# Projection stage of a one-core decoder step: value units on ScalarE, top-k rounds moved, first index scores earlier

## What is computed

```python
h = rmsnorm(x, g_mix)
proj = h @ w_in        # q_d,k_d,v_d | q_s,k_s,v_s | q_i,k_i,w_i | gates
q_d, k_d, q_s, k_s = rope(rmsnorm(per head of 64), pos)
q_i, k_i = rope(q_i, pos), rope(k_i, pos);  w_i = w_i * H_IDX ** -0.5
dots  = einsum('bqhd,bkd->bqhk', q_i, k_i) * DH_IDX ** -0.5
score = einsum('bqhk,bqh->bqk', relu(dots), w_i)    # causal
_, idx = top_k(score, 128)                          # of 512 (513) keys
```

## Time and profile before

| | us |
|---|---|
| median of 3 runs | 1186.04 (1186.01 to 1187.33) |
| the profiled execution | 1185.78 |
| its span, first to last instruction | 1184.0 |
| TensorE / VectorE / ScalarE / GpSimd busy | 1032.5 / 440.0 / 239.7 / 298.8 |
| projections, until TensorE's first instruction of the next stage | 289.28 |

### The profile page before, as it was taken

One profiled execution on the slowest core, in us unless ns is written; L12 is line 12 of the kernel. 1 busy time (PEld: TensorE's weight loads), 2 busy tenths in 40 slices (PEclk: granted clock), 3 DMA queues, 4 the chain that ended last, 5 costly groups with the idle time before them and its releaser, 6 DMA issues. The chain is left out here.

```text
span 1184.0 us, 16123 instructions
## 1 busy us (share of the span) xinstructions
PE 1032.5 (87%) x5989; PEld 576.3 (49%) x5989; DVE 440.0 (37%) x1213; ACT 239.7 (20%) x542; POOL 298.8 (25%) x262
## 2 busy tenths in 40 slices
PE   6998999988999999998999499999787777777775
PEld 3644443444777777332555355544444343444442
DVE  3635878786565574322334211111111011101220
ACT  2111212211444545301033201111100110011101
POOL 1033312441554434001000012322212221222111
PEclk9999999999999999998999789999999999999998
DMA  6232022107476444898391899999999999999991
GB/s 201 91 111 81 1 99 98 54 37 236 141 242 209 133 134 156 303 325 298 135 420 65 319 345 398 397 396 391 407 407 401 398 402 404 400 398 401 406 389 52
DMA packets 82465, 304.27 MB, mean 257 GB/s; under 512 B 23138, under 2 KB 27362, under 8 KB 70226
## 3 DMA queue, kind: packets, MB, share of 16 engines
q1 hardware_dynamic: 64658, 273.47, 60.6%
q0 software_dynamic: 9824, 16.98, 5.0%
q10 hardware_dynamic: 7904, 12.78, 3.0%
HBM read 290.09 MB, written 29.72 MB: 270 GB/s over the span
## 5 line engine op out<-in xcount | busy, mean ns | idle before, releaser
L383 PE MATMUL p_z<-k_w,k_xT 128*128 128x512 f32 (+2 forms) x528 | 212.3, 556 | 3.5 <-DVE p_t L584 3.4
L383 PEld LDWEIGHTS p_z<-k_w,k_xT 128*128 128x128 f32 (+1 forms) x528 | 93.1, 191 | 107.4 <-issue 106.7
L842 PE MATMUL a_G<-k_xT,k_w 128*128 128x260 f32 x512 | 127.3, 393 | 0.0
L2007 DVE TENSOR_TENSOR e_hid<-e_hid,e_G 128x256 f32<-128x256 f32 x32 | 13.5, 421 | 270.4 <-ACT e_hid L1920 263.2
L1925 ACT ACTIVATE e_y<-e_Y,x_share 64x512 f32<-64x512 f32 x64 | 43.7, 684 | 313.3 <-PE e_Y L1810 304.4
L842 PEld LDWEIGHTS a_G<-k_xT,k_w 128*128 128x128 f32 x512 | 93.2, 192 | 26.7 <-issue 13.8
L937 POOL TENSOR_TENSOR k_x<-k_x 128x512 f32<-128x512 f32 x64 | 80.5, 1272 | 89.6 <-DVE k_side L1003 66.0
L2048 POOL DMA_INDIRECT out_y_p<-e_y,x_table x32 | 45.1, 1408 | 202.8 <-ACT e_y L1925 144.1
L152 POOL DMA_INDIRECT k_rows<-token_rows,x_table x32 | 31.4, 981 | 179.1 <-PE e_TX L1790 169.6
L2012 DVE TENSOR_TENSOR e_hid<-e_hid,e_U 128x256 f32<-128x256 f32 x32 | 13.5, 421 | 126.1 <-PE e_U L1796 126.1
L1213 PE MATMUL g_ring<-k_oT,k_w 128*128 128x512 f32 x128 | 59.9, 614 | 0.0
(11 more groups left out here) (354 smaller groups left out, 1492.1 us busy)
## 6 DMA issues: line engine op xcount, KB each, us to landing
k_w<-in_w_in SPq DMA_DIRECT2D x11, 2048.0 KB, 8.5
k_xT<-in_w_down SPq DMA_DIRECT2D x11, 2048.0 KB
x_page<-in_w_down SPq DMA_DIRECT2D x10, 2048.0 KB
x_w_out<-in_w_down SPq DMA_DIRECT2D x10, 2048.0 KB
k_w<-in_w_gate SPq DMA_DIRECT2D x8, 2048.0 KB
k_w<-in_w_up SPq DMA_DIRECT2D x8, 2048.0 KB
k_oT<-in_w_gate SPq DMA_DIRECT2D x8, 2048.0 KB
k_side<-in_w_up SPq DMA_DIRECT2D x8, 2048.0 KB, 44.7
```

What stands on the lines that cost most here:

```text
L383: last = nc.tensor.matmul(z[u % 3][0:p, 0:WIDTH[k]], s.xT[:, j, 128 * i:128 * i + p], s.w[:, c % 2, j, 0:WIDTH[k]], start=j == 0, stop=j = ...
L842: last = nc.tensor.matmul(G[u % 2][:, 0:HT], s.w[:, q % 2, j, 128 * c:128 * c + 128], s.xT[:, j, HT * h:HT * h + HT], start=j == 0, stop=j ...
```

## The change

1. A value unit is copied out of its bank by ScalarE instead of VectorE (the sample unit straight into its row by four copies), and counted by a new semaphore `v_copied`. TensorE and SyncE wait for it where a value unit is meant; `z_free` now counts the other units only (`worked_before`).
2. A normalised prompt unit runs two rounds between its sums and its scaling, one behind the cosine product, none behind the unit.
3. A value prompt unit runs `2600 // (width + 128)` rounds (6, 5 or 4 at 256, 384, 512 columns), one less in a unit of `extras`.
4. The eight scores of t = 1 are made in units 10 and 11, four in each; those of t = 2 and 3 follow from unit 15 on, two in each.
5. `take_bank` waits for the relu that reads the bank (`relu_done`) instead of for VectorE's sum (`x_free`), outside the sample steps.
6. All four blocks are opened with `no_gpsimd_drain=True`: GpSimd's drain in front of the barrier is left out; the other engines drain by an instruction of their own ahead of the barrier's semaphores.

```diff
+def values_before(u):
+    return sum(k[0] == "v" for k, _ in UNITS[:u])
+def worked_before(u):
+    return u - values_before(u)
...
+BESIDE_VALUES = 2600
...
-        block = ctx.enter_context(nc.Block())
+        block = ctx.enter_context(nc.Block(no_gpsimd_drain=True))
...
+        EARLY = H
-        extras = {prompt_units[n // 2]: IDX_STEPS[n:n + 2] for n in range(0, len(IDX_STEPS), 2)}
+        extras = {prompt_units[n // 2]: IDX_STEPS[EARLY + n:EARLY + n + 2] for n in range(0, len(IDX_STEPS) - EARLY, 2)}
+        extras |= {IDX_FROM - 2: IDX_STEPS[0:EARLY // 2], IDX_FROM - 1: IDX_STEPS[EARLY // 2:EARLY]}
...
-                if 2 <= ne < PAIRS + 2:
-                    pe.wait_ge(kTi_ready, ne - 1)
-                elif ne >= PAIRS + 2:
-                    pe.wait_ge(x_free, ne - 1 - PAIRS)
+                before = ne - 2
+                if 0 <= before < EARLY:
+                    pe.wait_ge(relu_done, before + 1)
+                elif EARLY <= before < EARLY + PAIRS:
+                    pe.wait_ge(kTi_ready, before - EARLY + 1)
+                elif EARLY + PAIRS <= before < EARLY + X_SAMPLE:
+                    pe.wait_ge(x_free, before - EARLY - PAIRS + 1)
+                elif before >= 0:
+                    pe.wait_ge(relu_done, before - X_SAMPLE + 1)
...
                     if u >= 3:
-                        pe.wait_ge(z_free, u - 2)
+                        if UNITS[u - 3][0][0] == "v":
+                            pe.wait_ge(v_copied, values_before(u - 2))
+                        else:
+                            pe.wait_ge(z_free, worked_before(u - 2))
...
+                if UNITS[u][0][0] == "v":
+                    k, i = UNITS[u]
+                    act.wait_ge(proj, u + 1)
+                    if i < NT:
+                        last = nc.scalar.copy(s.v[k][:, i, :], z[u % 3][:])
+                    else:
+                        for g in range(NB):
+                            last = nc.scalar.copy(s.row[k][:, 128 * g:128 * g + 128], z[u % 3][32 * g:32 * g + NS, 0:128])
+                    last.then_inc(v_copied, 1)
...
-                if k[0] == "v":
-                    nc.vector.tensor_copy(s.v[k][:, i, :] if i < NT else s.row[k][:], bank[0:p, :]).then_inc(z_free, 1)
-                    dve.wait_ge(z_free, u + 1)
-                    dve.sem_inc(y_ready, 1)
-                    return
...
-                if k in NORMED and i < NT and rounds:
-                    take8(rounds.pop(0))
+                if k in NORMED and i < NT:
+                    for _ in range(min(2, len(rounds))):
+                        take8(rounds.pop(0))
...
-                for _ in range(0 if i == NT else 1 if k in NORMED else 5):
-                    if rounds:
+                if k[0] == "v" and i < NT and rounds:
+                    for _ in range(min(BESIDE_VALUES // (rounds[0].shape[1] + 128) - (u in extras), len(rounds))):
                         take8(rounds.pop(0))
```

More of the change, by code:

```diff
@@ L199, in project @@
              "relu_used wi_ready ptab_in pages_in kTi_ready ss_ready samp blk0 zs_ready newk_ready tb_ready").split())
+        v_copied = sem("v_copied")
         stored = [sem(f"stored{n}") for n in range(ROWS_KEPT)]
@@ L304, in _ @@
                 if k in STORED:
-                    sp.wait_ge(y_ready, u + 1)
+                    if k[0] == "v":
+                        sp.wait_ge(v_copied, values_before(u + 1))
+                    else:
+                        sp.wait_ge(y_ready, u + 1)
                     dst = io["new_%s_%s" % (out_of[k], "p" if i < NT else "s")]
@@ L389, in _ @@
                     pe.wait_ge(turn_out, turned_before(2 * TILES))
+                if u == IDX_FROM - 2:
+                    pe.wait_ge(turn_out, turned_before(TILES + 2))
                 for t, h in extras.get(u, ()):
@@ L437, in _ @@
                     nc.scalar.activation(lexp, lsum, ACT.Exp).then_inc(lam_exp, 1)
-                if u < U and UNITS[u][1] == NT and UNITS[u][0] != "kw":
+                if UNITS[u][0][0] == "v":
[3 more added lines that the diff above has]
+                        last = nc.scalar.copy(s.v[k][:, i, :], z[u % 3][:])
+                    else:
+                        for g in range(NB):
+                            last = nc.scalar.copy(s.row[k][:, 128 * g:128 * g + 128], z[u % 3][32 * g:32 * g + NS, 0:128])
+                    last.then_inc(v_copied, 1)
+                elif UNITS[u][1] == NT and UNITS[u][0] != "kw":
                     act.wait_ge(proj, u + 1)
@@ L475, in _ @@
                 for t, h in extras.get(u, ()):
-                    act.wait_ge(x_ready, X_SAMPLE + nx + 1)
+                    act.wait_ge(x_ready, use_of(nx) + 1)
                     if nx >= 2:
@@ L480, in _ @@
                     n = 128 * (t + 1)
-                    nc.scalar.activation(relu[:, nx % 2, 0:n], xs[(X_SAMPLE + nx) % 2][:, 0:n], ACT.Relu, scale=DH ** -0.5).then_inc(relu_done, 1)
+                    nc.scalar.activation(relu[:, nx % 2, 0:n], xs[use_of(nx) % 2][:, 0:n], ACT.Relu, scale=DH ** -0.5).then_inc(relu_done, 1)
                     nx += 1
@@ L557, in finish @@
                 bank = z[u % 3]
+                if k[0] == "v":
+                    dve.sem_inc(y_ready, 1)
+                    return
                 dve.wait_ge(proj, u + 1)
@@ L560, in finish @@
                     bank = zs
-                    dve.wait_ge(zs_ready, NB * sum(j == NT and q != "kw" for q, j in UNITS[:u + 1]))
+                    dve.wait_ge(zs_ready, NB * sum(j == NT and q != "kw" and q[0] != "v" for q, j in UNITS[:u + 1]))
                 if u >= ROWS_KEPT:
```

32 lines of the change are left out of this document (15 added, 17 removed).

## The result

The changed kernel took **1159.32 us** (median of 4 runs, 1159.26 to 1160.61) where the kernel before took 1186.68 us beside it (1186.01 to 1189.08): ratio 0.9765, 95% interval [0.975, 0.978]. The direction was right, the size was not.

A forecast was written before the change was run, and what follows sets the result against it. VectorE was taken to set the projections' pace from unit 16, TensorE close behind. TensorE's 19.9 us plus 1.6 at the stage's end gave 21.5 us, from 1186.04 to 1164.5 us; whole range 1160.5 to 1170.5.

The forecast's parts named there:

- Edits with no price: SyncE's wait for value copies and barriers without GpSimd's drain: 0 us, with 1.5 us at the program's end kept for the range.
- TensorE's stalls: Projections: idle time 12.7, stretched score matmuls 5.7 and clock 2.9 us go, 1.4 us of new stall comes: 19.9 us gained.
- VectorE out of the way: Projections: 26.4 us of VectorE's work and waits go, so it ends at 264.1 us, 0.9 before TensorE.
- early sums and rounds: VectorE, units 10 to 13: eight 256-column sums done early save 5.0 us, six rounds under GpSimd's answers 5.9 us.
- the copies: Value copies moved from VectorE to ScalarE, with the wait behind each: 7.5 us off VectorE.
- the holes: VectorE's idle time before scaling normalised prompt units, filled by two rounds: 9.4 of 10.4 us saved.
- The end of the stage: From TensorE's last projection matmul to the next stage: 2.8 us instead of 4.36, gain 1.6, VectorE's rounds and masks inside it.
- The clock of the next stage: TensorE behind the projections' barrier: a clock fall may vanish with shorter idle time; 1.5 us, kept for the range.
- VectorE as the bound: Rival, projections: VectorE still sets the pace, 1 us more per normalised unit, gain 11.6 us, 1174.4 us; 9%.
- lock each other out: Rival, normalised units: rounds and GpSimd's inverse root or sine product exclude each other, slower, 1200.9 us; 2%.
- time handed back: Rival, experts: first loads tied to something other than earlier stages, DMA absorbs half the gain, 1175 us; 4%.
- does not do what it says: Rival, score units: holes close but TensorE waits for ScalarE's relus, 2.7 us in each of eight units, 1186 us; 2%.

The follow-up runs named there:

- unit 34 alone: Changed kernel with one more round in each of the two holes of the samples' unit of the last queries only: 1156.95 us, ratio 0.9744.
- all sample holes: Changed kernel with one more round in each of the two holes of all k and q sample units: 1159.25 us.
- one round in the gap: Changed kernel with one round between sums and scaling and one behind the unit, as before the change: 1166.95 us.

## Why the prediction was wrong, point by point

- **The step that failed is "Edits with no price", the end of the program**: "Likely it ran beside SyncE's wait for that landing: 0, with 1.5 kept for the range". From the last issue to the end it was 8.2 us with the drain and 2.4 without, so 5.8 us stood on the path, and the edit alone, on the kernel before, gave 6.3 us by its rows and 6.5 by the medians. The bound of 1.5 rested on a landing at 1181.8 us, taken from the 9.12 us of two gathers. That chain step runs from the first issue to the end of both, with both issues inside it; the last scatters land 3.4 and 4.1 us from their issue in the changed kernel. The forecast's own low end, 1160.1 with that 1.5 in it, does not reach the measured time either. The windows of the kernel before held the answer: DMA share 0.00 from 1177 us on. With 5.8 in place of 0 the sum is 27.3 us, which gives 1158.7 us, 0.6 below the measured time. The 12 ns that the Trainium skill (VectorE: DVE Perf Modes, The DRAIN you can't avoid) gives for a boilerplate drain on any engine is not this one: GpSimd's took 0.5 us ahead of its first indirect DMA and 8.5 to 9.0 behind such DMAs.
- **TensorE's stalls**: forecast 19.9 us, measured 262.43 - 241.51 = 20.9. Idle time 12.7 and stretched scores 5.7 went as put; the projections' groups gave 3.6 (173.5 - 169.9) where 2.9 stood. The new stall was put at 1.4 us and is 1.3 to 1.5.
- **VectorE out of the way**: right, but not by the sum. It ended 3.3 us later than 264.1 once the 0.7 us of head start are taken off, for the sum only takes time away from VectorE's old course and has no place for a new wait: the 2.9 us in unit 25 are missing. And the 10.9 us credited to early sums and rounds were worth 1.5 us; the copies (7.5 put, 6.3 measured) and the holes (9.4 put, 8.1 measured) carry the gain.
- **The end of the stage**: "VectorE's rounds and masks end inside it" was wrong. VectorE was last by 1.5 us, and 0.57 us were gained instead of 1.6. This miss and the surplus on TensorE cancel: 20.9 + 0.6 = 21.5 us, the forecast of the stage to the digit, partly by luck.
- **Barrier at the inner ends, 0**: right. **The clock of the next stage**: unchanged, 0.57 in both.
- **Rivals.** VectorE as the bound (1174.4) came true only at the tail. GpSimd and VectorE did not lock each other out: the twelve scalings waited 1.2 us in all. The prediction's sign for time handed back, a stage behind the barrier that changes by more than 2 us, was just met: the merge lost 2.05 us, while the experts gave 0.75. It does not show that anything was handed back, for a second profile of the changed kernel has the merge at 199.79, 0.9 above the kernel before, and among all profiles, with the kernel before and its barrier included, the merge took 198.4 to 200.9 and the experts 501.9 to 504.7 us. That is scatter between runs; what causes it was not tried. That the kernel *does not do what it says* (TensorE waiting for ScalarE in the score units) is out: the scores from unit 15 on waited 0.0 us.

The chance of 95% for faster was sound; the range was too narrow by an edit that I had bounded by a row of another transfer.

## What to carry to other kernels

An instruction that no row shows, such as a drain at a block's end, is bounded by the silent time at that place, and a stretch at the end in which neither an engine nor a queue does anything is its price until shown otherwise; ask first which engine reaches the barrier last. When an engine is taken off the critical path, follow it to the stage's last instruction: its tail behind the last matmul counts in full even where its total has slack. Work moved earlier is worth only what the engine would not have fitted into its idle time anyway.

## What was not expected of the hardware

- A drain of GpSimd took 0.5 us where it had issued five plain loads, the last of them 100 us before, and no indirect DMA; it took 8.7 to 9.0 us behind 5 or 74 indirect DMAs. When all of these had landed it still took some 8.5 us, and the second of two in a row was free. Whether the kind of DMA or the time since the last one makes the difference was not tried.
- With 2.73 us of TensorE's idle time at the same barrier, the next stage's first 4 us ran at a granted clock of 1.00 once, 0.66 once and 0.57 once (unit 34 alone, all sample holes, one round in the gap); with 3.3 us and more it was 0.50 to 0.70. In the profiles at hand the attention then took 182.0 us against 183.5 to 185.0. By these profiles the clock behind a barrier can cost up to 3 us beside the idle time itself, and the length of that idle time alone does not tell whether it will.
